# Another order inside a page step of the sample attention of a two-layer decoder step

## The chip, the cores and the metric

The kernel runs on one core of a Trainium2 chip. What is measured is the time of one execution on the device, in microseconds (us). A core has a matrix engine (TensorE, PE in the rows, with its weight loads as PEld), VectorE (DVE), ScalarE (ACT), GpSimd (POOL), and SyncE (SP), which here only issues transfers. Each of the engines runs its own list of instructions from top to bottom; they meet through semaphores.

## The reference, cut to what matters

One inference step of two decoder layers, for a prompt of 2048 tokens and for 8 sample sequences of 4 new tokens each. The change touches the sample attention of layer 0, which for every sequence reads 16 pages of 128 cached keys and values through a page table:

```python
def fox_sample(q, k_new, v_new, lf_new, k_past, v_past, lf_past):
    ...
    s_past = jnp.einsum('bqhd,bkhd->bhqk', q, k_past).astype(jnp.float32) * scale
    s_past = s_past + suf[:, :, None, :] + c_new[:, :, :, None]
    s_new = jnp.einsum('bqhd,bkhd->bhqk', q, k_new).astype(jnp.float32) * scale
    ...
    p = jax.nn.softmax(jnp.concatenate([s_past, s_new], axis=-1), axis=-1).astype(v_new.dtype)
    out = (jnp.einsum('bhqk,bkhd->bqhd', p[..., :n_past], v_past)
           + jnp.einsum('bhqk,bkhd->bqhd', p[..., n_past:], v_new))
```

There are 8 heads of width 128, so a page of keys or of values is 128 x 1024 numbers, 512 KB, and there are 128 pages of each.

## The kernel before, in words

Every large product is computed in three terms: an operand x is split into a high part, x rounded to the format of the matrix engine (`_hi`), and the low rest (`_lo`). ScalarE casts the high part, VectorE subtracts it from x for the low part.

The sample attention (`sample_fox`) does not run by itself. It is dealt out between the matrix products of a projection pass, `project_pass` with the tag p01, which multiplies half the prompt by the 41 column tiles of `fox_w_in`. A tile has two chunks of 512 tokens, a chunk four slots, and a slot is 6 matmuls of line 365; so a tile is 8 slots and 48 matmuls. After each slot every engine's program calls `beside.advance(at)`, where `at` is the position in tiles, and runs as many steps of the side works as their plans say are due. A plan is a list of (position, steps due) with straight lines between. In p01 three side works share PSUM and one after the other do their steps: `sample_gates` (14 steps), `sample_fox` (153 steps, plan (2, 0) to (32, 153)) and `prompt_memory` (42 steps, (32, 0) to (41, 42)). Each engine writes out its own list by the same rule, so the order on an engine is fixed when the program is built; when it runs is a matter of the semaphores.

A step of `sample_fox` with index i has s = i - 3. Steps i = 0 to 2 load and prepare the queries, the new keys and the masks. From s = 0 on, one page of keys goes through per step, and from s = 19 on also one page of values:

- TensorE transposes the page's keys into two PSUM banks (line 1755); ScalarE copies them out as `kT_hi` (line 1774), VectorE makes `kT_lo` (line 1840). The next page's transposes and the scores wait for `kT_lo`.
- In every second step (s even) TensorE computes the scores of the two pages before (lines 1713 and 1714), 16 matmuls; ScalarE copies half of them (`low`, line 1781), VectorE adds them up in `sc` (lines 1855 and 1858).
- ScalarE casts `v_hi` (line 1804) and VectorE makes `v_lo` (line 1886) for the page of values that the next step multiplies: they loop over `products(s + 1)`. TensorE multiplies it in step s + 1 (lines 1734 and 1735, four matmuls). `v_hi` and `v_lo` have two halves, so a cast of page y waits for the products of page y - 2 (`pv_d`).

Inside a step, TensorE's order before is scores, products, transposes; ScalarE's and VectorE's is the key split, then the work on the scores, then the value split. Once per sequence, steps 16b + 16 to 16b + 20 add the softmax (a maximum over 2052 columns, an exponential, a normalisation), the transposes of the probabilities, and the copying out of the result; the last step of a sequence multiplies two pages, the 16th and the new tokens.

In the same lists stand the evictions of the projection (ScalarE, line 382, two per tile) and the split of the next tile's weights (VectorE, lines 338 and 340, once per tile). SyncE issues the loads of key pages (ring of four), of weights, the stores of z, and in step i = 1 twenty-four small loads for masks and biases; GpSimd issues the loads of value pages (ring of three), each when the split of the page three earlier is done.

Of the kernel before, what the change touches and what calls it, by code (L numbers as in the profile page):

```python
# [14 lines left out]
P = 128  # L15
# [1542 lines left out]
def sample_fox(nc, stack, room, const, banks, zT, gate_row, bT, cache_k, cache_v, page_table, sufT, cnew, cnew_q, v_new, plan, freed):  # L1558
# [131 lines left out]
    def pe(pe):  # L1690
        for i in range(STEPS):
            s = i - LEAD
            b = batch(s, 36)
            if b is not None:
                pe.wait_ge(o_d, 2 * b + 2)
                pe.wait_ge(ptl_d, min(2 * (b + 2), 2 * DB))
                for h in range(FH):
                    last = nc.tensor.matmul(M_BANK[:, h * LO:(h + 1) * LO], o_sb[:, h * P:(h + 1) * P], eye2[:, :], start=True, stop=True)
                last.then_inc(x_d, 1)
            if group(s) is not None:  # L1700
                b, g = group(s)
                if b == 0 and g == 0:
                    pe.wait_ge(zero_d, 3)
                    pe.wait_ge(eye_d, 1)
                    pe.wait_ge(kn_d, 2)
                pe.wait_ge(qx_d, 2 * b + 2)
                pe.wait_ge(ktl_d, 2 * s)
                if s > 2:
                    pe.wait_ge(hi_d, NG * b + g + b)
                    pe.wait_ge(low_d, NG * b + g + b)  # L1710
                for h in range(FH):
                    q = qx[:, h * P:(h + 1) * P]
                    nc.tensor.matmul(S_BANK[:, 0:2 * P], q, kT_hi[:, h, :], start=(h == 0), stop=False)
                    last = nc.tensor.matmul(S_BANK[:, 0:2 * P], q, kT_lo[:, h, :], start=False, stop=(h == FH - 1))
                if g == NG - 1:
                    out = S_BANK[:, 2 * P:2 * P + TN]
                    for h in range(FH):
                        q = qx[:, h * P:(h + 1) * P]
                        nc.tensor.matmul(out, q, kn_hi[:, h, TN * b:TN * (b + 1)], start=(h == 0), stop=False)
                        last = nc.tensor.matmul(out, q, kn_lo[:, h, TN * b:TN * (b + 1)], start=False, stop=(h == FH - 1))  # L1720
                last.then_inc(s_done, 1)
            for b, p in products(s):
                y = NV * b + p
                if p == 0:
                    pe.wait_ge(ptl_d, 2 * b + 1)
                    if b:
                        pe.wait_ge(o_d, 2 * b)
                if p == PAGES:
                    pe.wait_ge(ptl_d, 2 * b + 2)
                pe.wait_ge(vl_d, y + 1)  # L1730
                pr = pT[:, p * 2 * LO:p * 2 * LO + P]
                for n in range(2):
                    vs = slice(n * 512, (n + 1) * 512)
                    nc.tensor.matmul(O_BANKS[n][:, :], pr, v_hi[:, y % 2, vs], start=(p == 0), stop=False)  # L1734
                    last = nc.tensor.matmul(O_BANKS[n][:, :], pr, v_lo[:, y % 2, vs], start=False, stop=(p == PAGES))
                last.then_inc(pv_d, 1)
            b = batch(s, 18)
            if b is not None:
                pe.wait_ge(pn_d, b + 1)
                if b >= 2:  # L1740
                    pe.wait_ge(m_d, b - 1)
                for p in range(PAGES):
                    last = nc.tensor.transpose(M_BANK[:, p * LO:p * LO + R], sc[0:R, b % 2, p * P:(p + 1) * P], ident[0:R, 0:R])
                last.then_inc(pt_d, 1)
            b = batch(s, 19)
            if b is not None:
                pe.wait_ge(ptl_d, 2 * b + 1)
                nc.tensor.transpose(M_BANK[:, 0:R], sc[0:R, b % 2, W:W + P], ident[0:R, 0:R]).then_inc(pt_d, 1)
            if 0 <= s < NPG:
                pe.wait_ge(k_in[s % KR], 16 * (s // KR + 1))  # L1750
                if s:
                    pe.wait_ge(ktl_d, 2 * s)
                for n in range(2):
                    for h in range(4):
                        last = nc.tensor.transpose(T_BANKS[n][:, h * P:(h + 1) * P], k_raw[:, s % KR, (4 * n + h) * P:(4 * n + h + 1) * P], ident[:, :])  # L1755
                    last.then_inc(kt_d, 1)
            yield

    def packed(t, first, n, off):
# [2 lines left out]
    def act(act):  # L1762
        for i in range(STEPS):
            s = i - LEAD
            if i == 1:
                act.wait_ge(set_in, 32)
                nc.scalar.activation(qs_hi[:, :, :], q_raw[:, :, :], ACT.Copy, scale=SCALE).then_inc(set_d, 1)
                act.wait_ge(zero_d, 3)
            if 0 <= s < NPG:
                for n in range(2):  # L1770
                    act.wait_ge(kt_d, 2 * s + n + 1)
                    if s % 2 == 0 and s and n == 0:
                        act.wait_ge(s_done, s // 2)
                    nc.scalar.copy(kT_hi[:, 4 * n:4 * n + 4, s % 2 * P:(s % 2 + 1) * P],  # L1774
                                   T_BANKS[n][:, :].rearrange("p (h n) -> p h n", h=4)).then_inc(kth_d, 1)
# [20 lines left out]
            if b is not None:  # L1796
                act.wait_ge(pt_d, 2 * b + 2)
                nc.scalar.copy(packed(pT, PAGES, 1, 0), M_BANK[:, 0:LO].rearrange("p (n r) -> p n r", r=LO)).then_inc(pth_d, 1)
            for b, p in products(s + 1):
                y = NV * b + p  # L1800
                act.wait_ge(v_in[y % VR], 16 * (y // VR + 1))
                if y >= 2:
                    act.wait_ge(pv_d, y - 1)
                nc.scalar.copy(v_hi[:, y % 2, :], v_raw[:, y % VR, :]).then_inc(vh_d, 1)
# [9 lines left out]
    def dve(dve):  # L1814
        def diag(off):
            return qx[:, off:off + FH * (P + TN)].rearrange("p (h x) -> p h x", x=P + TN)[:, :, 0:TN]
        for i in range(STEPS):
# [8 lines left out]
            if i == 2:  # L1826
                dve.wait_ge(kn_in, 16 * (1 + 3 * FH))
                nc.vector.tensor_copy(kn_hi[:, :, :], kn_raw[:, :, :]).then_inc(kn_d, 1)
                dve.wait_ge(kn_d, 1)
                nc.vector.tensor_tensor(kn_lo[:, :, :], kn_raw[:, :, :], kn_hi[:, :, :].bitcast(F32), ALU.subtract).then_inc(kn_d, 1)  # L1830
                nc.vector.tensor_tensor(c_bias[:, :, :], c_qry[:, :].unsqueeze(2).broadcast_to([R, DB, TN]), c_key[:, :, :], ALU.subtract).then_inc(bias_d, 1)
                dve.wait_ge(bias_d, 1)
                nc.vector.tensor_tensor(c_bias[:, :, :], c_bias[:, :, :], mask[:, :].unsqueeze(1).broadcast_to([R, DB, TN]), ALU.add).then_inc(bias_d, 1)
                dve.wait_ge(bias_d, 2)
                dve.wait_ge(set_d, 2)
            if 0 <= s < NPG:
                for n in range(2):
                    at = (slice(None), slice(4 * n, 4 * n + 4), slice(s % 2 * P, (s % 2 + 1) * P))
                    dve.wait_ge(kth_d, 2 * s + n + 1)
                    nc.vector.tensor_tensor(kT_lo[at], T_BANKS[n][:, :].rearrange("p (h n) -> p h n", h=4),  # L1840
                                            kT_hi[at].bitcast(F32), ALU.subtract).then_inc(ktl_d, 1)
# [37 lines left out]
            if b is not None:  # L1879
                dve.wait_ge(pth_d, 2 * b + 2)  # L1880
                nc.vector.tensor_tensor(packed(pT, PAGES, 1, LO), M_BANK[:, 0:LO].rearrange("p (n r) -> p n r", r=LO),
                                        packed(pT, PAGES, 1, 0).bitcast(F32), ALU.subtract).then_inc(ptl_d, 1)
            for b, p in products(s + 1):
                y = NV * b + p
                dve.wait_ge(vh_d, y + 1)
                nc.vector.tensor_tensor(v_lo[:, y % 2, :], v_raw[:, y % VR, :], v_hi[:, y % 2, :].bitcast(F32), ALU.subtract).then_inc(vl_d, 1)  # L1886
# [287 lines left out]
def decoder_step(nc, ins, outs):  # L2174
# [18 lines left out]
    with ExitStack() as s:  # L2193
# [28 lines left out]
        with ExitStack() as s0:  # L2222
# [13 lines left out]
            with ExitStack() as s1:  # L2236
                hi, lo = half_states(0, 1, s1, xp, xs, norm_pre[0])

                def works(stack, landed):
                    with ExitStack() as room:  # L2240
                        gates, ends_g = sample_gates(nc, stack, room, const, banks[2:8], z0, F_ROW, fox_b_f, past, fox_lf_s, sufT,
                                                     cnew, cnew_q, fox_k_s, fox_v_s, [(0, 0), (2, 14)])
                    with ExitStack() as room:
                        fox, ends_f = sample_fox(nc, stack, room, const, banks[2:8], z0, 3 * D + XW, bT, cache_k, cache_v, page_table,
                                                 sufT, cnew, cnew_q, fox_v_s.rearrange("b t h d -> (b t) (h d)"),
                                                 [(2, 0), (32, 153)], ends_g)
                    prompt, _ = prompt_memory(0, stack, stack, z0, 3 * D, 3 * D + XW + D, [(32, 0), (41, 42)],
                                              lambda sp: landed(sp, XQ - 1), ends_f)
                    return [gates, fox, prompt]
                project_pass(nc, "p01", banks, fox_w_in, hi, lo, z0, tiles, CHUNKS[1], STORES[1], works)  # L2250
# [49 lines left out]
```

## Time and profile before

| | before |
|---|---|
| median of 3 runs | 4248.09 us (4244.42 to 4254.1) |
| profiled execution, its own time | 4249.62 us |
| its span in the trace | 4248.1 us |
| TensorE matmul busy | 3629.0 us, 85% of the span |
| VectorE busy | 1889.8 us, 44% |
| ScalarE busy | 1317.4 us, 31% |
| GpSimd busy | 335.5 us, 8% |
| granted TensorE clock, mean of the run | 0.924 |

The span is the trace's from the first instruction to the last. Busy shares are means over stages with different limits; the pass p01 lies between about 726 and 1893 us of the span. The granted clock is a share of full speed: 1.00 is 2.4 GHz, and 0.5 is the lower of the two levels, 1.2 GHz.

### The profile page before, as it was taken

To read this page: it belongs to the slowest core of one execution; us is meant where nothing else is said; L and a number is where in the kernel's file an instruction comes from. 1 tells how busy PE (TensorE), PEld (TensorE's weight loads), DVE (VectorE), ACT (ScalarE), POOL (GpSimd) and SP (SyncE) were. 2 spreads that over 40 slices of the span, in tenths; PEclk is the share of its full clock that TensorE was granted. 3 is DMA by queue.
4 is the path that set the end of the run, shared out by engine and by line. 5 is a ranking of instruction groups with operands and counts; after the bars stand their busy time and mean duration, and the time that the engine had idled before them with its cause. 6 is when DMAs were issued, how large, how long until landed. Compare 5 with 4: busy or idle time off the path is not lost. (4 is left out here: it accounts for less than half of the span.)

```text
span 4248.1 us, 56572 instructions
## 1 busy us (share of the span) xinstructions
PE 3629.0 (85%) x19825; PEld 3133.0 (74%) x19825; DVE 1889.8 (44%) x3378; ACT 1317.4 (31%) x2438; POOL 335.5 (8%) x549
## 2 busy tenths in 40 slices
PE   5699995788888889988888888599689779997899
PEld 4699995677777677766777777488589767775687
DVE  3311323255455555445666666533321144574433
ACT  1211212244333434334545555211211144411111
POOL 0131000000000001000101111000000000122000
PEclk8799997999999999998999999799899989998899
DMA  4333332565555555322222222333222243474432
GB/s 143 93 89 108 120 97 84 164 192 179 172 174 180 184 184 180 120 96 101 99 92 89 82 82 82 106 104 108 83 91 91 89 130 113 131 223 157 133 113 76
DMA packets 385337, 523.94 MB, mean 123 GB/s; under 512 B 52855, under 2 KB 275064, under 8 KB 380495
## 3 DMA queue, kind: packets, MB, share of 16 engines
q1 hardware_dynamic: 317255, 398.72, 30.1%
q0 software_dynamic: 30624, 93.22, 6.7%
q10 hardware_dynamic: 37248, 29.37, 2.2%
q8 instruction: 112, 1.84, 0.2%
q14 instruction: 98, 0.80, 0.1%
HBM read 388.83 MB, written 132.74 MB: 123 GB/s over the span
## 5 line engine op out<-in xcount | busy, mean ns | idle before, releaser
L382 ACT ACTIVATE z_st_p<-bank 128x352 f32<-128x352 f32 (+3 forms) x325 | 167.8, 518 | 728.6 <-PE bank L365 727.9
L1333 PE MATMUL bank<-w_hi_o,b_hi_o 128*128 128x512 f32 x816 | 328.3, 402 | 70.3 <-DVE w_lo_o L1375 70.3
L1840 DVE TENSOR_TENSOR kT_lo_sf<-bank,kT_hi_sf 128x512 fp32r<-128x512 f32 x256 | 167.0, 687 | 379.6 <-ACT kT_hi_sf L1774 379.4
L365 PE MATMUL bank<-h00hi,w_hi_p 128*128 128x352 f32 x984 | 319.9, 325 | 11.3 <-DVE w_lo_p L340 7.7
L338 DVE CAST w_hi_p<-w_raw_p 128x1024 fp32r<-128x1024 f32 (+1 forms) x130 | 89.3, 687 | 529.7 <-PE bank L365 509.8
L1334 PE MATMUL bank<-w_hi_o,b_lo_o 128*128 128x512 f32 x816 | 324.1, 397 | 0.0
L1335 PE MATMUL bank<-w_lo_o,b_hi_o 128*128 128x512 f32 x816 | 323.9, 397 | 0.0
L365 PE MATMUL bank<-h00hi,w_lo_p 128*128 128x352 f32 x984 | 316.7, 322 | 0.0
L365 PE MATMUL bank<-h00lo,w_hi_p 128*128 128x352 f32 x984 | 316.6, 322 | 0.0
L1774 ACT CAST kT_hi_sf<-bank 128x512 fp32r<-128x512 f32 x256 | 140.1, 589 | 514.1 <-PE bank L1755 513.7
L365 PE MATMUL bank<-h01hi,w_hi_p 128*128 128x512 f32 x656 | 284.5, 434 | 8.9 <-DVE w_lo_p L340 8.9
L365 PE MATMUL bank<-h01lo,w_hi_p 128*128 128x512 f32 x656 | 262.5, 400 | 0.0
L365 PE MATMUL bank<-h01hi,w_lo_p 128*128 128x512 f32 x656 | 262.1, 399 | 0.0
L1333 PEld LDWEIGHTS bank<-w_hi_o,b_hi_o 128*128 128x128 f32 x816 | 156.3, 192 | 117.9 <-DVE w_lo_o L1375 44.3
L751 DVE TENSOR_TENSOR pT_lo_fa<-bank,pT_hi_fa 128x512 fp32r<-128x512 f32 (+2 forms) x320 | 194.1, 609 | 103.6 <-ACT pT_hi_fa L692 102.5
L645 PE MATMUL bank<-pT_hi_fa,v_hi_fa 128*128 128x256 f32 x576 | 182.8, 317 | 58.9 <-DVE mix_fa L726 50.6
L1734 PE MATMUL bank<-v_hi_sf,pT_sf 128*128 128x512 f32 x272 | 124.6, 458 | 107.8 <-DVE v_lo_sf L1886 107.7
L742 DVE CUSTOM_DVE_ANT_0 sc_fa<-bank,decay_fa 128x512 f32<-128x512 f32 (+2 forms) x320 | 193.3, 604 | 51.2 <-PE bank L625 26.4
L692 ACT CAST pT_hi_fa<-bank 128x512 fp32r<-128x512 f32 (+2 forms) x320 | 162.2, 515 | 145.5 <-PE bank L659 145.5
L697 ACT ACTIVATE sc_fa<-sc_fa,nm_fa 128x128 f32<-128x128 f32 (+15 forms) x128 | 154.2, 1205 | 148.6 <-DVE nm_fa L756 148.1
L365 PEld LDWEIGHTS bank<-h00hi,w_hi_p 128*128 128x128 f32 x984 | 185.6, 189 | 12.7 <-DVE w_lo_p L340 7.9
L365 PE MATMUL bank<-h10hi,w_hi_p 128*128 128x352 f32 x576 | 187.1, 325 | 7.1 <-DVE w_lo_p L340 7.1
(359 smaller groups left out, 8833.6 us busy)
## 6 DMA issues: line engine op xcount, KB each, us to landing
z<-z_st_p SPq DMA_DIRECT2D x128, 512.0 KB, 2.7
k_raw_sf<-in_cache_fox_k SPq DMA_DIRECT2D x128, 512.0 KB, 4.0
v_raw_sf<-in_cache_fox_v POOLq DMA_DIRECT2D x128, 512.0 KB, 3.9
w_raw_p<-in_fox_w_in SPq DMA_DIRECT2D x80, 512.0 KB, 5.1
b_raw_o<-bT SPq DMA_DIRECT2D x32, 768.0 KB, 7.4
w_raw_p<-in_pool_w_in SPq DMA_DIRECT2D x48, 512.0 KB, 4.7
out<-tok_fa ACTq DMA_DIRECT2D x64, 256.0 KB, 2.3
w_raw_o<-in_w_out ACTq DMA_DIRECT2D x24, 512.0 KB, 3.9
```

What stands on the lines that cost most here:

```text
L365: last = nc.tensor.matmul(out, wt[:, u, k, :], h[:, k, at0:at0 + width], start=(m == 0), stop=(m == MM - 1))
L382: nc.scalar.activation(z_st[0:rows, t % 2, at0:at0 + width], banks[n % 2][0:rows, 0:width], func).then_inc(z_read, 1)
L645: nc.tensor.matmul(out, v_hi[:, n, :], ph, start=(n == 0), stop=False)
L692: nc.scalar.copy(pT_hi[:, jt % 2, 4 * p:4 * p + nk, a * P:(a + 1) * P], T_BANKS[g % 2][:, 0:nk * P].rearrange("p (n q) -> p n q", q=P)).th ...
L697: nc.scalar.activation(sc[:, qs % NB, 0:w], sc[:, qs % NB, 0:w], ACT.Exp, bias=nm[:, qs % NB:qs % NB + 1], accum_out=rs[:, qs // QB % 2, q ...
L742: nc.vector.tensor_tensor_reduce(out=sc[:, b, k0:k0 + w], in0=S_BANKS[g % 4][:, 0:w], in1=decay[:, k0:k0 + w], scale=1.0, scalar=LOWEST, o ...
L751: nc.vector.tensor_tensor(pT_lo[at], T_BANKS[g % 2][:, 0:nk * P].rearrange("p (n q) -> p n q", q=P), pT_hi[at].bitcast(F32), ALU.subtract) ...
L1333: nc.tensor.matmul(out, bh, w_hi[:, k, cols], start=(k == 0), stop=False)
L1334: nc.tensor.matmul(out, bl, w_hi[:, k, cols], start=False, stop=False)
L1335: last = nc.tensor.matmul(out, bh, w_lo[:, k, cols], start=False, stop=(k == NK - 1))
L1774: nc.scalar.copy(kT_hi[:, 4 * n:4 * n + 4, s % 2 * P:(s % 2 + 1) * P], T_BANKS[n][:, :].rearrange("p (h n) -> p h n", h=4)).then_inc(kth_d, 1)
L1840: nc.vector.tensor_tensor(kT_lo[at], T_BANKS[n][:, :].rearrange("p (h n) -> p h n", h=4), kT_hi[at].bitcast(F32), ALU.subtract).then_inc(k ...
```

## The change

On TensorE the transposes of a step now stand between the scores and the products. On ScalarE and VectorE the split of the first page of values of `products(s + 1)` now stands at the head of the step, ahead of the key split; the second page, which there is once per sequence, stays where it was. The plans change too: the gates end at 1.8 tiles in place of 2, the three preparing steps of `sample_fox` are spread over tiles 2 to 4 and the other 150 over tiles 4 to 33, and `prompt_memory` begins at 33 in place of 32. No instruction is added or taken away.

```diff
@@ sample_fox, pe(pe): after the scores, ahead of the products
+            if 0 <= s < NPG:
+                pe.wait_ge(k_in[s % KR], 16 * (s // KR + 1))
+                if s:
+                    pe.wait_ge(ktl_d, 2 * s)
+                for n in range(2):
+                    for h in range(4):
+                        last = nc.tensor.transpose(T_BANKS[n][:, h * P:(h + 1) * P], k_raw[:, s % KR, (4 * n + h) * P:(4 * n + h + 1) * P], ident[:, :])
+                    last.then_inc(kt_d, 1)
             for b, p in products(s):
                 y = NV * b + p
...
@@ sample_fox, pe(pe): the same eight lines go from the end of the step
-            if 0 <= s < NPG:
-                pe.wait_ge(k_in[s % KR], 16 * (s // KR + 1))
...
@@ sample_fox, act(act): ahead of the key split
+            for b, p in products(s + 1)[0:1]:
+                y = NV * b + p
+                act.wait_ge(v_in[y % VR], 16 * (y // VR + 1))
+                if y >= 2:
+                    act.wait_ge(pv_d, y - 1)
+                nc.scalar.copy(v_hi[:, y % 2, :], v_raw[:, y % VR, :]).then_inc(vh_d, 1)
...
-            for b, p in products(s + 1):
+            for b, p in products(s + 1)[1:]:
...
@@ sample_fox, dve(dve): ahead of the key split
+            for b, p in products(s + 1)[0:1]:
+                y = NV * b + p
+                dve.wait_ge(vh_d, y + 1)
+                nc.vector.tensor_tensor(v_lo[:, y % 2, :], v_raw[:, y % VR, :], v_hi[:, y % 2, :].bitcast(F32), ALU.subtract).then_inc(vl_d, 1)
...
-            for b, p in products(s + 1):
+            for b, p in products(s + 1)[1:]:
...
@@ decoder_step, the plans of the side works of p01
-                                                     cnew, cnew_q, fox_k_s, fox_v_s, [(0, 0), (2, 14)])
+                                                     cnew, cnew_q, fox_k_s, fox_v_s, [(0, 0), (1.8, 14)])
...
-                                                 [(2, 0), (32, 153)], ends_g)
+                                                 [(2, 0), (4, 3), (33, 153)], ends_g)
...
-                    prompt, _ = prompt_memory(0, stack, stack, z0, 3 * D, 3 * D + XW + D, [(32, 0), (41, 42)],
+                    prompt, _ = prompt_memory(0, stack, stack, z0, 3 * D, 3 * D + XW + D, [(33, 0), (41, 42)],
```

On TensorE, a step without scores between two slots of the projection (`h01` and `w_hi_p` are the projection's operands) stood so before:

```order
L365 MATMUL bank<-h01hi,w_lo_p 128x512
L1734 MATMUL bank<-v_hi_sf,pT_sf 128x512
L1735 MATMUL bank<-v_lo_sf,pT_sf 128x512
L1734 MATMUL bank<-v_hi_sf,pT_sf 128x512
L1735 MATMUL bank<-v_lo_sf,pT_sf 128x512
L1755 MATMUL bank<-ident_const,k_raw_sf 128x128 x8
L365 MATMUL bank<-h01hi,w_hi_p 128x512
```

The same step on TensorE now:

```order
L365 MATMUL bank<-h01hi,w_lo_p 128x512
L1728 MATMUL bank<-ident_const,k_raw_sf 128x128 x8
L1742 MATMUL bank<-v_hi_sf,pT_sf 128x512
L1743 MATMUL bank<-v_lo_sf,pT_sf 128x512
L1742 MATMUL bank<-v_hi_sf,pT_sf 128x512
L1743 MATMUL bank<-v_lo_sf,pT_sf 128x512
L365 MATMUL bank<-h01hi,w_hi_p 128x512
```

The eight transposes of the page of keys have moved ahead of the four products.

On ScalarE, in the middle of a sequence, a step without scores and one with them stood so before (line 382 is an eviction of the projection):

```order
L1774 CAST kT_hi_sf<-bank 128x4x128 x2
L1804 CAST v_hi_sf<-v_raw_sf 128x1024
L1774 CAST kT_hi_sf<-bank 128x4x128 x2
L1781 COPY low_sf<-bank 32x256
L1804 CAST v_hi_sf<-v_raw_sf 128x1024
L382 ACTIVATE z_st_p<-bank 128x512
```

And two such steps there now:

```order
L382 ACTIVATE z_st_p<-bank 128x512
L1774 CAST v_hi_sf<-v_raw_sf 128x1024
L1780 CAST kT_hi_sf<-bank 128x4x128 x2
L1787 COPY low_sf<-bank 32x256
L1774 CAST v_hi_sf<-v_raw_sf 128x1024
L1780 CAST kT_hi_sf<-bank 128x4x128 x2
```

The cast of the values has moved from the end of a step to its head; VectorE's subtraction of the values moves with it.

On VectorE, at the start of `sample_fox` (`kn` is the new keys, `c_bias` the bias with the mask, lines 338 and 340 the split of a weight tile), the list was:

```order
L1828 CAST kn_hi_sf<-kn_raw_sf 128x256
L1830 TENSOR_TENSOR kn_lo_sf<-kn_raw_sf,kn_hi_sf 128x256
L1831 TENSOR_TENSOR c_bias_sf<-c_qry_sf,c_key_sf 32x32
L1833 TENSOR_TENSOR c_bias_sf<-c_bias_sf,mask_sf 32x32
L1840 TENSOR_TENSOR kT_lo_sf<-bank,kT_hi_sf 128x4x128 x4
L1846 CAST qx_sf<-qs_hi_sf 128x8x4
L1847 CAST qx_sf<-qs_lo_sf 128x8x4
L338 CAST w_hi_p<-w_raw_p 128x1024
L340 TENSOR_TENSOR w_lo_p<-w_raw_p,w_hi_p 128x1024
```

It is now:

```order
L1834 CAST kn_hi_sf<-kn_raw_sf 128x256
L1836 TENSOR_TENSOR kn_lo_sf<-kn_raw_sf,kn_hi_sf 128x256
L1837 TENSOR_TENSOR c_bias_sf<-c_qry_sf,c_key_sf 32x32
L1839 TENSOR_TENSOR c_bias_sf<-c_bias_sf,mask_sf 32x32
L338 CAST w_hi_p<-w_raw_p 128x1024
L340 TENSOR_TENSOR w_lo_p<-w_raw_p,w_hi_p 128x1024
L1850 TENSOR_TENSOR kT_lo_sf<-bank,kT_hi_sf 128x4x128 x4
L1856 CAST qx_sf<-qs_hi_sf 128x8x4
L1857 CAST qx_sf<-qs_lo_sf 128x8x4
```

A weight split now stands between the preparing step and the first key split; on TensorE, 204 matmuls of the projection stand ahead of the first page's transposes where 138 stood, and 12 between the first and the second page's transposes where 6 stood.

## Rows read from the trace of the kernel before

**Rows 1.** Windows of the span: engine busy us (instructions), granted clock, DMA share, GB/s.

```profile
800.00:900.00 100.00, 94.45 (x591) 80.61 (x591) 50.89 (x84) 39.62 (x72) 2.11 (x4) 1.00 0.57 176
900.00:920.00 20.00, 18.26 (x101) 14.83 (x100) 13.28 (x18) 8.92 (x15) 1.59 (x3) 1.00 0.76 239
900.00:1640.00 740.00, 632.01 (x3464) 523.86 (x3463) 383.85 (x540) 295.07 (x471) 59.34 (x112) 0.93 0.58 180
...
1720.00:1893.00 173.00, 164.60 (x842) 132.27 (x840) 87.72 (x145) 68.80 (x194) 16.65 (x16) 1.00 0.35 113
```

**Rows 2.** Waits of TensorE, 720 to 1893 us: total us, times, longest.

```profile
PE bank L1734 <- DVE v_lo_sf L1886: 107.7, 63, 3.3
PE bank L1755 <- DVE kT_lo_sf L1840: 15.9, 5, 14.8
...
PE bank L1755 <- DMA k_raw_sf<-in_cache_fox_k: 6.8, 1, 6.8
PE bank L942 <- ACT pr_ma L1005: 4.8, 5, 1.0
```

**Rows 3.** TensorE in order of time, 1134 to 1147.3 us: start, duration, instruction.

```profile
1134.13 1.03 PE L1755 MATMUL bank<-ident_const,k_raw_sf 128*128 128x128 f32 x8
1134.92 0.48 PE L365 MATMUL bank<-h01hi,w_hi_p 128*128 128x512 f32 x1
...
1137.76 0.28 PE L1713 MATMUL bank<-kT_hi_sf,qx_sf 128*128 128x256 f32 x1
...
1139.67 0.40 PE L1734 MATMUL bank<-v_hi_sf,pT_sf 128*128 128x512 f32 x1
...
1140.61 1.04 PE L1755 MATMUL bank<-ident_const,k_raw_sf 128*128 128x128 f32 x8
...
1145.17 0.50 PE L1734 MATMUL bank<-v_hi_sf,pT_sf 128*128 128x512 f32 x1 [2.13 <-DVE v_lo_sf L1886]
```

**Rows 4.** ScalarE in the same stretch.

```profile
1134.77 1.07 ACT L1774 CAST kT_hi_sf<-bank 128x512 fp32r<-128x512 f32 x2 [2.56 <-PE bank L1755]
1135.73 1.06 ACT L1804 CAST v_hi_sf<-v_raw_sf 128x1024 fp32r<-128x1024 f32 x1
...
1142.35 0.36 ACT L1781 COPY low_sf<-bank 32x256 f32<-32x256 f32 x1
```

**Rows 5.** VectorE in the same stretch.

```profile
1135.39 1.29 DVE L1840 TENSOR_TENSOR kT_lo_sf<-bank,kT_hi_sf 128x512 fp32r<-128x512 f32 x2 [2.34 <-ACT kT_hi_sf L1774]
...
1143.07 0.46 DVE L1855 SCALAR_TENSOR_TENSOR sc_sf<-sc_sf,c_qry_sf,bank 32x256 f32<-32x256 f32 x1
...
1143.91 1.21 DVE L1886 TENSOR_TENSOR v_lo_sf<-v_raw_sf,v_hi_sf 128x1024 fp32r<-128x1024 f32 x1
```

**Rows 6.** TensorE in order of time, 1052 to 1060 us.

```profile
1054.82 0.50 PE L1734 MATMUL bank<-v_hi_sf,pT_sf 128*128 128x512 f32 x1 [2.12 <-DVE v_lo_sf L1886]
...
1057.91 0.63 PE L365 MATMUL bank<-h01lo,w_hi_p 128*128 128x512 f32 x1
1058.34 0.63 PE L365 MATMUL bank<-h01hi,w_lo_p 128*128 128x512 f32 x1
```

**Rows 7.** TensorE, then VectorE, where the sample attention starts.

```profile
777.81 1.97 PE L1755 MATMUL bank<-ident_const,k_raw_sf 128*128 128x128 f32 x8 [6.80 <-DMA k_raw_sf<-in_cache_fox_k]
...
797.15 1.94 PE L1755 MATMUL bank<-ident_const,k_raw_sf 128*128 128x128 f32 x8 [14.80 <-DVE kT_lo_sf L1840]
...
794.62 0.29 DVE L1828 CAST kn_hi_sf<-kn_raw_sf 128x256 fp32r<-128x256 f32 x1 [18.95 <-DMA c_qry_sf<-cnew_q]
...
800.51 0.68 DVE L338 CAST w_hi_p<-w_raw_p 128x1024 fp32r<-128x1024 f32 x1
801.23 1.22 DVE L340 TENSOR_TENSOR w_lo_p<-w_raw_p,w_hi_p 128x1024 fp32r<-128x1024 f32 x1
```

**Rows 8.** Casts of the pages of values, and their loads' time to landing.

```profile
L1804 ACT CAST v_hi_sf<-v_raw_sf x136: 1027/1048/1076, 878.2 to 1697.4; 128x1024 fp32r<-128x1024 f32 x136
...
DMA to landing us min/median/max: 2.1/3.9/8.6
```

More of the change, by code:

```diff
@@ L1748, in pe @@
                 nc.tensor.transpose(M_BANK[:, 0:R], sc[0:R, b % 2, W:W + P], ident[0:R, 0:R]).then_inc(pt_d, 1)
-            if 0 <= s < NPG:
-                pe.wait_ge(k_in[s % KR], 16 * (s // KR + 1))
[L1751 to L1756, printed above, removed]
             yield
```

## The prediction

> **What bounds the kernel now.** The change touches only the pass p01, so I read that stretch. First the table of windows [rows 1]: while pages of keys and values are worked on, from 900 to 1640 us, TensorE is busy for 632.01 of 740 us, against 383.85 for VectorE and 295.07 for ScalarE, and the granted clock is 0.93. From 800 to 900 us, where mostly keys are worked on, it is busy for 94.45 of 100 us at 1.00. So TensorE is the bound, and it loses time in two ways: 108 us of standing idle, and a clock that is at times at the lower of its levels.
>
> Then the table of TensorE's waits [rows 2] says for whom it stands idle: 107.7 us in 63 waits of the value products (line 1734) for the low part of the values. The waits of line 1755, 15.9 us for VectorE (14.8 of them in one wait) and 6.8 us for a page of keys, belong to the start of the work. Together these three lines hold 130 us. Last, the order of time over two steps [rows 3 to 5] shows why: the transposes start at 1134.13, the key split keeps ScalarE from 1134.77 on and VectorE from 1135.39 on, and only behind it come the casts of the values. With a step of two slots and scores the products still start on time (1139.67); in the next step, which has one slot and no scores, they stand for 2.13 us until the subtraction that starts at 1143.91 is done.
>
> **What the lower clock costs.** After a wait of 2.12 us [rows 6] projection matmuls follow each other at 0.43 us; at full speed twelve take 2.84 us with the changeover (1134.92 to 1137.76, rows 3), 0.24 us each. 0.43 is the 1.2 GHz level, 0.24 the 2.4 GHz one. A mean clock of 0.93 over 740 us is 2 x 0.07 x 740 = 104 us at the lower level, of which, if all were work, half, 52 us, is lost. That is the upper bound of what can come back; the lower is 0. I take 30: some of the 104 us is idle, and some waits will remain.
>
> **The change in a steady step, walked with these durations** [rows 3 to 5]. Let transposes start at T. They take 0.79 us to the next instruction, products 0.94 (1139.67 to 1140.61), a slot 1.42 (half of 2.84), scores 1.91. The key split ends on ScalarE at T + 1.71 (0.64 + 1.07) and on VectorE at T + 2.55 (1.26 + 1.29).
>
> Before, the value cast follows on ScalarE (0.36 later if there is a copy of scores), and VectorE's subtraction of 1.21 after the score additions: that subtraction ends at T + 4.5 in the step shown (1143.91 + 1.21 - 1140.61), and TensorE, with one slot and no scores, is at the products at T + 0.79 + 1.42 = T + 2.2. The 2.3 between are the wait of 2.13.
>
> Now the products of step s take values split in step s - 1, so they follow the transposes at once. The next thing that can wait is the next transposes or scores, which need the key split: T + 2.55 against T + 0.79 + 0.94 + 1.42 = T + 3.15 at the earliest. 0.6 us is left. The cast at the head of the next step may start when these products end, T + 1.73, and after ScalarE's key split and copy of scores (about T + 2.1); it ends at T + 3.2. VectorE adds up scores until about T + 3.4, subtracts until T + 4.6, and would be wanted for the next key split at T + 3.15 + 1.26 = T + 4.4. It is 0.2 us late, out of 0.6. A weight split, once per tile, puts 0.68 + 1.22 = 1.9 us in front [rows 7], which makes it 2.1 us late; but the plan gives 232 slots to 150 steps, 1.55 per step, so of two neighbouring steps at least one has two slots, and its 1.42 and the 0.6 cover this but for 0.1. In the steady steps I count the wait as gone.
>
> Once per sequence it is not gone. In step 16b + 18 the first cast is for the next sequence's first page, and its buffer is free only when the products of the 16th old page are done, which TensorE does behind this very step's transposes: T + 0.79 + 0.94 = T + 1.73. The key split behind the cast then starts at T + 1.73 + 1.06 = T + 2.8 in place of T + 0.64, 2.1 us late, and with the copies and the softmax of the same steps two or three later waits of 0.3 to 0.7 us appear. I take 2.5 us per sequence, 20 us for 8; bounds 5 and 64, the latter if every second step waited 1 us as well.
>
> So of 107.7 us, 20 stay: 87.7 gained, and 30 from the clock.
>
> **The start.** The first key split on VectorE stands behind the preparing step, which waits for small loads until 794.62 [rows 7]. These are issued by SyncE when the gates' room is free, so they come hardly earlier; TensorE stood without work meanwhile. It was free of waits until 777.81 - 6.80 = 771.0. With 66 more matmuls (204 against 138) ahead of the first transposes, 15.6 us at 0.237, they start at 786.6, the page has long landed, and with 12 matmuls behind it TensorE stands at the second transposes at about 790.3. VectorE gets there after the small loads and now after a weight split too: 797.15 + 1.9 = 799.1, a wait of about 9 in place of 6.8 + 14.8. By then TensorE has done 72 matmuls more than before at the same place (66 + 6), worth 17.1 us, and is 1.9 us later: 15 us gained; bounds 5 (the small loads come 10 us later, behind the weight load and the store now ahead of them on SyncE's list) and 21.6 (no wait left).
>
> **The end.** `prompt_memory` does its 42 steps in 8 tiles in place of 9. TensorE waits there for 4.8 us on ScalarE now, and is busy for 164.60 of 173 us [rows 1, 2]. Denser steps leave less between: I add 4 us, bounds 0 and 10. The matmuls of the projection are only dealt out otherwise; no instruction is new. The loads of keys (SyncE's list) keep their place against the transposes; those of values are issued when the value split is done, whose cover is below. The earlier end of the gates' plan moves two slots of 1.42 us at most and I count nothing.
>
> **Sum.** -107.7 + 20 - 30 - 15 + 4 = -128.7 us against the profiled execution's 4249.6: 4120.9, 4121 us. That execution lies 1.5 us over the median of the runs, within their spread of 9.7 us; 0.2% or 8.5 us is about what a measurement can tell from no change.
>
> **Rivals.**
> 1. *The cast at the head holds the key split in many steps.* Against it: the walk, with 0.6 us to spare. For it: ScalarE and VectorE have evictions and weight splits in the same lists, and 0.6 us is little. If every second of 128 steps waits 1 us, 64 stay in place of 20, and half of the clock's share: -107.7 + 64 - 15 - 15 + 4 = -70, 4180 us. Decided by whether the key split ends later than T + 3.15. The Trainium skill's "TensorE: Matmul & The Clock Gate" (section "Architectural detail: the array is 16× 32×32, not 1× 128×128") says that the queues of ScalarE and VectorE are strictly first in, first out, so that nothing behind a waiting cast can pass it; it speaks for this rival. By the rule alone the sum would go to 4180; by the rows the cast waits for products that end before the next transposes start, except once per sequence, and it stays at 4121.
> 2. *The clock does not come back.* The waits go, but TensorE's dips stay, as with the 0.93 of today: 0 in place of 30, 4151 us. Against it: 1.00 from 800 to 900 us with the same instructions but the products.
> 3. *All of it comes back*: 5 us of waits left, 50 from the clock, 2 at the end: -107.7 + 5 - 50 - 15 + 2 = -166, 4084 us.
> 4. *Slower: pages of values come too late.* The load of a page is issued when the split of the page three earlier is done, and the cast at the head then holds the key split, and with it all of TensorE, until the page lands. Steps now last (1697.4 - 878.2) / 128 = 6.4 us [rows 8], afterwards some 5.5; cover is 3 x 5.5 less the cast's 1.06 and the subtraction's 1.21, 14 us. It decides from there on: with 17.5 us to landing, a step lasts 6.6, and 128 steps 26 us more, less 15 at the start and 4 back: 4265 us. Against it: loads land in 3.9, at most 8.6 us, and the engines moved 239 GB/s in one stretch, against 180 now [rows 1] and some 180 x 6.4 / 5.5 = 210 then.
>
> **Chances.** The forecast 0.55 (its own range 4095 to 4145), rival 1 0.17, rival 2 0.13, rival 3 0.11, rival 4 0.04. The predicted time is that of the forecast. The range from 4080 to 4185 takes in rivals 1 to 3 with the bounds of the waits and of the clock, and leaves out rival 4 and more waits than rival 1 has. Faster by over 0.2% are the first four cases but for a part of rival 1 that goes far beyond its price: 0.93; within 0.2% 0.03; slower 0.04.
>
> **What would show it.** In the waits of TensorE: line 1742 on `v_lo` nearly gone; some 20 us on `kT_lo` (lines 1713 and 1728), at the same steps of every sequence, and one of about 9 us at the start; nothing on pages of values by ScalarE but at the sequences' ends. The granted clock of the stretch at 0.97 or more, TensorE's busy share there at 0.95 or more. Wrong it would be made by many waits of 0.3 to 1 us on `kT_lo` (rival 1), by a clock of 0.93 without idle time (rival 2), or by ScalarE's casts waiting for loads (rival 4).

## The result, and the profile after

| | before | changed |
|---|---|---|
| median, runs taken together | 4249.83 us (4 runs, 4244.42 to 4254.1) | 4075.64 us (4 runs, 4065.68 to 4077.56) |
| ratio, 95% interval | | 0.9586 (0.9567 to 0.9605) |
| profiled execution | 4249.62 us | 4075.30 us |
| span | 4248.1 us | 4073.8 us |

The change makes the kernel 174 us faster; 4121 was predicted, in a range from 4080, so the sign is right, the size is not, and the time lies below the range.

The head of the changed kernel's page, with its span in 40 slices (granted clock and transfers):

```profile
span 4073.8 us, 56573 instructions
...
PE 3561.2 (87%) x19825; PEld 3098.8 (76%) x19825; DVE 1884.2 (46%) x3378; ACT 1320.7 (32%) x2438; POOL 336.6 (8%) x549
...
PEclk8799998899999999989999998899799799997899
...
GB/s 137 98 98 98 126 95 90 146 199 243 232 216 240 236 201 113 102 82 106 103 83 90 96 86 46 127 116 88 91 95 95 85 124 122 157 215 167 114 108 79
```

TensorE's busy time falls from 3629.0 to 3561.2 us with the same 19825 instructions. The slices from the eighth to the seventeenth are the pass p01: from the ninth on the clock is at 9, and in the ninth to the fifteenth the transfers run at 199 to 243 GB/s.

The windows table over the whole pass, of the kernel before and then of the changed one; the pass ends at 1892.0 and at 1713.3 us, so each window is the pass, rounded up to a us. The columns are those of [rows 1].

```profile
726.00:1893.00 1167.00, 1020.08 (x5489) 840.35 (x5489) 573.65 (x833) 444.78 (x791) 92.63 (x158) 0.94 0.54 167
```

```profile
726.00:1714.00 988.00, 955.40 (x5489) 808.88 (x5489) 568.04 (x832) 447.65 (x791) 93.38 (x158) 0.99 0.62 197
900.00:1640.00 740.00, 722.57 (x4218) 616.04 (x4217) 457.63 (x650) 360.35 (x610) 78.10 (x137) 1.00 0.66 210
```

This pair of rows splits the gain. The pass is 179 us shorter (1167 and 988). TensorE's idle time falls from 146.9 (1167 - 1020.08) to 32.6 us, by 114.3; its busy time for the same 5489 instructions falls by 64.7. The rest of the span, 4248.1 - 1893 and 4073.8 - 1714, is within 5 us the same. In the stretch of [rows 1] the clock goes from 0.93 to 1.00 and the busy time from 632.01 to 722.57 of 740 us.

Not all of the 64.7 us is the clock. Summed over windows of 5 us, the granted clock stands at the lower level for 128 us of the pass before and for 19 us of it now; half of the difference, 55 us, is the most that the clock can have given back. The other 10 us or so fit the ends of matmuls in front of a wait. These two rows of the kernel before stand ahead of the wait of 2.13 us in [rows 3]:

```profile
1142.41 0.39 PE L365 MATMUL bank<-h01lo,w_hi_p 128*128 128x512 f32 x1
1142.64 0.40 PE L365 MATMUL bank<-h01hi,w_lo_p 128*128 128x512 f32 x1
```

A matmul's row lasts 0.39 to 0.40 us, but the next one starts 0.23 us after it. The last one before a wait therefore counts as busy for some 0.16 us in which TensorE would already have begun the next; for the 63 waits of [rows 2] that is an estimated 10 us.

TensorE's waits in the pass, the answer to [rows 2]:

```profile
PE bank L1728 <- DVE kT_lo_sf L1850: 12.3, 6, 10.8
...
PE bank L942 <- ACT pr_ma L1005: 8.2, 9, 1.0
PE bank L1713 <- DVE qx_sf L1857: 4.4, 7, 0.8
PE bank L1742 <- DVE v_lo_sf L1896: 1.4, 1, 1.4
...
PE bank L1742 <- DVE pT_sf L1886: 1.1, 4, 0.3
```

The 107.7 us on `v_lo` are gone but for 1.4 and a 0.5 that is not shown. One wait of 10.8 us at the start is left of 21.6, and `prompt_memory` waits 8.2 in place of 4.8.

A step of one slot without scores, the kind that lost 2.13 us in [rows 3], with the scores behind it: TensorE, then VectorE.

```profile
1151.86 1.04 PE L1728 MATMUL bank<-ident_const,k_raw_sf 128*128 128x128 f32 x8
1152.65 0.48 PE L1742 MATMUL bank<-v_hi_sf,pT_sf 128*128 128x512 f32 x1
...
1153.67 0.40 PE L365 MATMUL bank<-h01hi,w_hi_p 128*128 128x512 f32 x1
...
1155.06 0.28 PE L1713 MATMUL bank<-kT_hi_sf,qx_sf 128*128 128x256 f32 x1
```

```profile
1152.26 1.23 DVE L1845 TENSOR_TENSOR v_lo_sf<-v_raw_sf,v_hi_sf 128x1024 fp32r<-128x1024 f32 x1 [1.46 <-ACT v_hi_sf L1774]
1153.40 1.28 DVE L1850 TENSOR_TENSOR kT_lo_sf<-bank,kT_hi_sf 128x512 fp32r<-128x512 f32 x2
```

The products start 0.79 us after the transposes (1152.65) because `v_lo` was made in the step before. The key split of 1.28 us that starts at 1153.40 ends at 1154.68; the slot's six matmuls start at 1153.67 and last, at 0.23 us each, until 1155.06, where the scores follow at once. 0.4 us of slack is left, and nothing waits.

### The profile page after: what moved, and what is told of

It is laid out like the page before. It is cut to its first block and busy times, and to the rows that moved or that the text cites. A ratio compares the mean times of both kernels' runs of the same rounds, so it can differ in the third digit from the quotient of the medians.

```text
span 4073.8 us, 56573 instructions
## 1 busy us (share of the span) xinstructions
PE 3561.2 (87%) x19825; PEld 3098.8 (76%) x19825; DVE 1884.2 (46%) x3378; ACT 1320.7 (32%) x2438; POOL 336.6 (8%) x549
## 5 line engine op out<-in xcount | busy, mean ns | idle before, releaser
L365 PE MATMUL bank<-h01hi,w_hi_p 128*128 128x512 f32 x656 | 269.2, 410 | 9.0 <-DVE w_lo_p L340 9.0
L659 PE MATMUL bank<-ident_const,sc_fa 128*128 128x128 f32 x1088 | 176.1, 279 | 20.6 <-ACT sc_fa L697 13.9
```

Source lines behind the costliest of these rows:

```text
L365: last = nc.tensor.matmul(out, wt[:, u, k, :], h[:, k, at0:at0 + width], start=(m == 0), stop=(m == MM - 1))
L659: last = nc.tensor.transpose(T_BANKS[g % 2][:, n * P:(n + 1) * P], sc[:, qt % NB, (4 * p + n) * P:(4 * p + n + 1) * P], ident[:, :])
```

## The experiments

Two theories. A: TensorE lost time because too little work lay between what releases a split and what needs it; either move gives the missing cover, and the clock had fallen behind those waits. The rivals: B, only the two moves together carry it; C, the clock's share has another cause, such as the plans. The pass's rows are read from windows tables as above.

| run | median us | ratio to before (95%) | pass us | TensorE busy | idle | clock 900 to 1640 |
|---|---|---|---|---|---|---|
| before | 4249.83 | 1 | 1167 | 1020.1 | 146.9 | 0.93 |
| changed | 4075.64 | 0.9586 (0.9567 to 0.9605) | 988 | 955.4 | 32.6 | 1.00 |
| plans only | 4246.99 | 0.9981 (0.9971 to 0.9990) | 1161 | 1023.8 | 137.2 | 0.93 |
| order only | 4086.04 | 0.9594 (0.9578 to 0.9610) | 1001 | 960.8 | 40.2 | 0.99 |
| transposes first only | 4100.65 | 0.9630 (0.9614 to 0.9646) | 1011 | 962.2 | 48.8 | 0.99 |
| values first only | 4107.26 | 0.9645 (0.9629 to 0.9661) | 1021 | 967.0 | 54.0 | 0.99 |
| changed, again | 4074.49 | 0.9579 (0.9566 to 0.9592) | 990 | 956.6 | 33.4 | 1.00 |
| wait in every 4th step | 4147.51 | 0.9750 (0.9732 to 0.9768) | 1066 | 975.3 | 90.7 | 0.97 |
| wait in every 2nd step | 4261.05 | 1.0019 (1.0007 to 1.0031) | 1179 | 1015.7 | 163.3 | 0.93 |

**Plans or order.** The first run is the kernel before with the three plan lines of the change, the second the changed kernel with the three plan lines of before:

```diff
@@ e1: before.py
-  [(0, 0), (2, 14)]       [(2, 0), (32, 153)]           [(32, 0), (41, 42)]
+  [(0, 0), (1.8, 14)]     [(2, 0), (4, 3), (33, 153)]   [(33, 0), (41, 42)]
@@ e2: after.py
-  [(0, 0), (1.8, 14)]     [(2, 0), (4, 3), (33, 153)]   [(33, 0), (41, 42)]
+  [(0, 0), (2, 14)]       [(2, 0), (32, 153)]           [(32, 0), (41, 42)]
```

> The kernel before with the three new plans and nothing else. Theory A (TensorE lost time to the waits for the values, and its clock fell behind these waits; the plans only save waits at the start): the wait of the value products stays at about 105 us, the granted clock of the stretch 900 to 1640 at about 0.93, only the start's 21.6 us fall to about 11; 4235 us. Rival C (the clock's gain came from the other start and the other spread of the steps): clock near 1.00 in that stretch in spite of the waits, 4190 us or less.

> The changed kernel with the three old plans: the order of the change alone. Theory A: the value waits are gone and the clock is near 1.00, while the start's waits of about 20 us are back; some 12 us over the changed kernel, 4088 us. Rival C: clock back near 0.93, 4130 us or more.

The kernel before took 4255.16 us beside these runs (median of 13). The plans alone give 8 us, the order alone 169. For the plans alone A had 4235 us, and 4246.99 was measured: TensorE's idle time fell by 9.7 us, as expected of the start, but its busy time rose by 3.7. The waits of the run with the plans alone:

```profile
PE bank L1734 <- DVE v_lo_sf L1886: 106.0, 62, 4.7
PE bank L1755 <- DVE kT_lo_sf L1840: 13.2, 5, 12.1
```

106.0 us on the values stay, and the clock stays at 0.93. C falls as far as the plans go: the clock comes back with the order and does not come back without it.

**One move at a time.** The third run moves only TensorE's transposes, the fourth only the value split:

```diff
@@ e3: after.py, act and dve as before the change
-            for b, p in products(s + 1)[0:1]:
...
-            for b, p in products(s + 1)[1:]:
+            for b, p in products(s + 1):
@@ e4: after.py, pe as before the change: the transposes go back behind the products
-            if 0 <= s < NPG:
-                pe.wait_ge(k_in[s % KR], 16 * (s // KR + 1))
...
```

> The changed kernel with ScalarE's and VectorE's order of before: only TensorE's transposes are moved. Theory A (what counts is how much TensorE has to do between the transposes, which release the splits, and the value products): moving the products behind the next transposes gives the value split 0.8 to 1.7 us more; it ends at 3.9 to 4.6 us after the start of the transposes before, and the products are reached at 3.9 us at the earliest; some 20 us of waits for v_lo stay, in steps of one slot, 4105 us. Rival B (the value split must also stand first, or the key split before it holds it): half of the waits stay, about 50 us, and half of the clock's loss, 4155 us or more.

> The changed kernel with TensorE's order of before: only the value split stands first on ScalarE and VectorE. Theory A: the value split of the next page is then done before this step's transposes release the key split, so the products never wait; the scores and the next transposes follow the transposes by 2.2 us at the earliest and need the key split at 2.55 us, so some 10 to 25 us of waits for kT_lo appear, 4100 us. Rival B (only with the transposes first is there cover): waits for kT_lo of 60 us or more, 4165 us or more.

The waits of TensorE that remain, with the transposes first only:

```profile
PE bank L1742 <- DVE v_lo_sf L1886: 24.2, 30, 2.9
```

and with the values first only:

```profile
PE bank L1713 <- DVE qx_sf L1857: 9.9, 7, 1.5
...
PE bank L1713 <- issue: 8.1, 23, 0.7
PE bank L1734 <- DVE pT_sf L1886: 7.1, 7, 1.6
```

Each move alone gives 148 to 155 us, near what A's walk gave (4105 and 4100) and far from B's 4155 and 4165. With the transposes first, 24.2 us of waits on `v_lo` are left, 20 were expected. With the values first, there are the waits that the walk did not name: on `qx`, on `pT` and on TensorE's own issue, 25 us, and only a us beside the start's on `kT_lo`, where 10 to 25 were expected. So they are two ways to the same cover, and the second of them adds some 20 to 30 us.

**Waits put back.** In the changed kernel the products of every fourth step also wait for the key split of the same step; in the second run it is every second step, with `p % 2 == 0`:

```diff
                 pe.wait_ge(vl_d, y + 1)
+                if p % 4 == 2 and s < NPG:
+                    pe.wait_ge(ktl_d, 2 * s + 2)
                 pr = pT[:, p * 2 * LO:p * 2 * LO + P]
```

> The changed kernel, in which the value products of every fourth step also wait for the key split of the same step: 32 waits of about 1.8 us, 57 us in all, put back on purpose. Theory A (the clock falls behind such waits, and before each us of wait cost 0.57 us of slower work: 64.8 us for 113.6): 57 + 32 = 89 us, 4165 us. Rival C (the clock's loss of before has another cause): 57 us, 4132 us, with the granted clock of the stretch at 0.99.

> The same in every second step: 64 waits of about 1.8 us, 115 us, as much as was taken away. Theory A: 115 + 65 = 180 us, 4255 us, with a granted clock of about 0.93. Rival C: 4190 us, with a clock of 0.99.

TensorE's waits for the key split ahead of the products, in the first and in the second run:

```profile
PE bank L1744 <- DVE kT_lo_sf L1852: 59.9, 27, 4.2
```

```profile
PE bank L1744 <- DVE kT_lo_sf L1852: 133.5, 61, 4.2
```

The windows table of the second run, the pass and the stretch, and three rows of TensorE in order of time from it:

```profile
728.00:1907.00 1179.00, 1015.66 (x5489) 848.23 (x5489) 571.34 (x833) 450.27 (x791) 92.80 (x158) 0.94 0.53 165
900.00:1640.00 740.00, 610.82 (x3383) 517.83 (x3382) 373.06 (x528) 291.13 (x457) 59.89 (x111) 0.93 0.57 180
```

```profile
1103.45 0.76 PE L1744 MATMUL bank<-v_hi_sf,pT_sf 128*128 128x512 f32 x1 [3.74 <-DVE kT_lo_sf L1852]
...
1108.28 0.63 PE L365 MATMUL bank<-h01hi,w_lo_p 128*128 128x512 f32 x1
1108.71 0.63 PE L365 MATMUL bank<-h01hi,w_hi_p 128*128 128x512 f32 x1
```

No work is added, yet TensorE is busy for 59 us more than in the changed kernel run again (1015.66 against 956.6), beside 130 us more of idle time; the clock is at 0.93 again, and behind a wait projection matmuls follow each other at 0.43 us (1108.28 and 1108.71), the 1.2 GHz level. With half as many waits it is 18.7 us beside 57.3. The median, 4261.05 us, is near A's 4255 and far from C's 4190. This is A's order of things, waits first and the clock behind them. A's price of 0.57 us per us of wait holds only for the kernel it was read from: it is 0.33 in the one run, 18.7 / 57.3, and 0.45 in the other, which is why every fourth step came out at 4147.5 us and not at 4165. By the estimate above, some 4 of the 18.7 us and 10 of the 59 are the ends of matmuls ahead of the waits; the rest goes with the clock.

**The end of a sequence, and the start.** Three value buffers let the cast at the head of a step go without waiting for products; for the room the ring of keys goes from four to three pages and the output shares the query's buffer. In the other run VectorE's wait for the small loads moves behind the first key splits, to just ahead of the first score additions:

```diff
@@ e7
-    KR, VR = 4, 3
+    KR, VR = 3, 3
-    v_hi, v_lo = (c.sb(n, [P, 2, D], F32R) for n in ("v_hi", "v_lo"))
+    v_hi, v_lo = (c.sb(n, [P, 3, D], F32R) for n in ("v_hi", "v_lo"))
+    out_all = q_raw
...
-                if y >= 2:
-                    act.wait_ge(pv_d, y - 1)
+                if y >= 3:
+                    act.wait_ge(pv_d, y - 2)
@@ e6, dve: the block from the wait on kn_in to the wait on bias_d
-            if i == 2:
+            if s == 2:
                 dve.wait_ge(kn_in, 16 * (1 + 3 * FH))
...
@@ e6, pe
-                    pe.wait_ge(kn_d, 2)
...
                 if g == NG - 1:
+                    if b == 0:
+                        pe.wait_ge(kn_d, 2)
```

> The changed kernel again, as the base for the two runs beside it: 4075 us within 0.2%.

> The changed kernel with three in place of two buffers for v_hi and v_lo, so that the cast at the head of a step never waits for the products of the step itself; for the room the ring of keys has three pages in place of four and the output shares the query's buffer. The prediction's step (at a sequence's end the head cast holds the key split, 2.5 us per sequence, 20 us): 4055 to 4060 us. Rival, by the trace of the changed kernel (the hold is covered by the second page's products and the transposes of the probabilities): no change, 4075 us within 4.

> The changed kernel, with VectorE's wait for the small loads (and the split of the new keys and the bias behind it) moved from the preparing step to just before the first score additions, and TensorE's wait for the new keys to their first use. Theory A (the wait of 10.8 us at the start is VectorE standing at the small loads ahead of the first key split): that wait goes, some of it comes back two steps later at the first scores; 4075 - 8 = 4067 us. Rival (the first key split is late for another reason, such as the key page or the weight split): no change, 4075 us.

> The kernel with the later wait for the new keys once more, because its time fell by 13 us while the pass it touches took only 3 us less. If those 13 us belong to the kernel: 4061 us within 4. If they were of that chip and hour: about 4070 us.

> Both small changes, the later wait for the new keys and three value buffers. If the two gains are separate and real (13 and 6 us): 4056 us. If only what the pass shows is real (3 and 4 us): 4067 us.

| run | median us | ratio to before (95%) | pass us | behind the pass us |
|---|---|---|---|---|
| changed, again | 4074.49 | 0.9579 (0.9566 to 0.9592) | 990 | 2354 |
| three value buffers | 4068.78 | 0.9561 (0.9548 to 0.9574) | 986 | 2356 |
| later wait | 4061.49 | 0.9548 (0.9535 to 0.9561) | 987 | 2347 |
| later wait, again | 4064.64 | 0.9560 (0.9544 to 0.9576) | 986 | 2350 |
| both | 4059.11 | 0.9549 (0.9533 to 0.9566) | 976 | 2350 |

Three buffers give 6 us, not the 15 to 20 that the hold was priced at: ScalarE's cast at a sequence's end no longer waits (1131.08) and the key split starts at the transposes (1133.16),

```profile
1131.08 1.04 ACT L1775 CAST v_hi_sf<-v_raw_sf 128x1024 fp32r<-128x1024 f32 x1
1133.16 1.08 ACT L1781 CAST kT_hi_sf<-bank 128x512 fp32r<-128x512 f32 x2 [1.03 <-PE bank L1729]
```

but the pass is only 4 us shorter, and behind the start TensorE's waits are much the same: 1.5 us on `kT_lo` in both runs, 4.4 and 4.3 us on `qx`. The intervals of the two ratios overlap, so the 6 us are little more than the runs can tell from nothing. With the later wait, the wait at the start goes from 11.5 us (changed, again) to 6.3:

```profile
PE bank L1729 <- DVE kT_lo_sf L1843: 7.8, 6, 6.3
```

What holds the 6.3 us is no longer the small loads. The weight split, which the change put ahead of the first key split on VectorE, waits for its own load:

```profile
793.15 0.69 DVE L338 CAST w_hi_p<-w_raw_p 128x1024 fp32r<-128x1024 f32 x1 [14.39 <-DMA w_raw_p<-in_fox_w_in]
...
795.02 1.28 DVE L1843 TENSOR_TENSOR kT_lo_sf<-bank,kT_hi_sf 128x512 fp32r<-128x512 f32 x2
```

So the theory and its rival each hold in part here.

Behind the pass is the span less the end of the pass's window. Both together have the lowest median, 4059.11 us, but the ratio is that of the later wait alone (0.9549 and 0.9548), so the runs do not show that the two gains add up. In the one trace of both, the pass is 14 us shorter than that of the changed kernel run again, more than the 3 or 4 of each alone. The medians of the later wait lie 10 to 13 us under the changed kernel's 4074.49, though one of the first four runs of the changed kernel also took only 4065.68; the pass accounts for 3 to 4 of them. The others lie behind the pass, in stages that the edit does not touch, where the three runs with it take 2347 to 2350 us and the other two 2354 and 2356. What does that was not found.

## Why the prediction was wrong

**What bounds the kernel**, right: waits for `v_lo`, too little cover, in the place named. The transposes-first and values-first runs show that more cover, of either kind, takes most of these waits away: 24.2 and about 3 us on `v_lo` are left of 107.7.

**The steady step**, right: 0.6 us of slack was enough. After 880 us the profile lists no wait on `kT_lo`, and VectorE's weight splits were absorbed, as in the walk.

**The sequence's end**, wrong: "I take 2.5 us per sequence, 20 us for 8". These 20 us were to be waits on `kT_lo`, and the profile lists none there; about 8 us are left in the pass on `qx`, `pT` and `v_lo` together. The mechanism is there, only hardly anybody waits for it. ScalarE, VectorE and TensorE at such a step:

```profile
1132.53 1.05 ACT L1774 CAST v_hi_sf<-v_raw_sf 128x1024 fp32r<-128x1024 f32 x1 [3.40 <-PE bank L1743]
1133.48 1.06 ACT L1780 CAST kT_hi_sf<-bank 128x512 fp32r<-128x512 f32 x2
```

```profile
1134.75 1.28 DVE L1850 TENSOR_TENSOR kT_lo_sf<-bank,kT_hi_sf 128x512 fp32r<-128x512 f32 x2
```

```profile
1130.47 1.03 PE L1728 MATMUL bank<-ident_const,k_raw_sf 128*128 128x128 f32 x8
...
1133.29 1.18 PE L1751 MATMUL bank<-ident_const,sc_sf 32*128 32x32 f32 x16
...
1137.26 1.03 PE L1728 MATMUL bank<-ident_const,k_raw_sf 128*128 128x128 f32 x8
```

The cast waits for the products until 1132.53 and the key split starts only behind it, at 1133.48, though all transposes, from 1130.47 on, are long done. The Trainium skill ("TensorE: Matmul & The Clock Gate", section "Architectural detail: the array is 16× 32×32, not 1× 128×128") states that the queues of ScalarE and VectorE are strictly first in, first out; these rows agree, 1133.48 behind 1132.53. VectorE ends the key split at 1136.03, T + 5.6 with T the start of the transposes, 3.0 us later than in the steady walk; I had 2.1. But in the same step TensorE does a second page's products, the sixteen transposes of the probabilities (1133.29) and two slots before it wants the key split, at 1137.26, T + 6.8 in place of T + 3.15. I followed the split's lateness through ScalarE and VectorE and did not lay TensorE's own extra work of the same step against it: 3.0 us late met 3.6 us more of cover and the 0.6 of slack. Where such a step has one slot, as from 958.79 to 964.50, TensorE stands idle for 0.1 us. Rival 1, the same hold in many steps, did not appear either.

**The clock**, wrong, and the larger part: "That is the upper bound of what can come back; the lower is 0. I take 30". TensorE's busy time fell by 64.7 us. Two terms were mis-sized. Of the clock's 52 nearly all came back: 128 us of the pass at the lower level became 19, and half of the difference is 55 us, in a pass of which the bound counted only 900 to 1640 us. I took little more than half, though my own walk took the waits away. The idle part was a reason to take less, but a small one: by the rows TensorE stood idle for some 16 of the 128 us. The other 10 us or so are a term that I put at nothing, the ends of the matmuls ahead of the waits; it stood in my own walk, as the 2.3 us from need to end beside a wait of 2.13. The runs with waits put back show that the slower work belongs to the waits; that the ends of matmuls are what the clock leaves over is an estimate.

**The start**, right: the first page's transposes at about 786, the second at 800.02 after a wait of 10.78 us; predicted were 786.6, 799.1 and 9. What VectorE does ahead of it, and TensorE's wait:

```profile
795.63 0.29 DVE L1834 CAST kn_hi_sf<-kn_raw_sf 128x256 fp32r<-128x256 f32 x1 [17.64 <-DMA c_qry_sf<-cnew_q]
...
797.45 1.23 DVE L340 TENSOR_TENSOR w_lo_p<-w_raw_p,w_hi_p 128x1024 fp32r<-128x1024 f32 x1
798.59 1.28 DVE L1850 TENSOR_TENSOR kT_lo_sf<-bank,kT_hi_sf 128x512 fp32r<-128x512 f32 x2
```

```profile
800.02 1.94 PE L1728 MATMUL bank<-ident_const,k_raw_sf 128*128 128x128 f32 x8 [10.78 <-DVE kT_lo_sf L1850]
```

The order without the plans is 10 us slower than the changed kernel by the medians, and its pass 13 us longer (1001 and 988); in the sum the plans stood for 15 less 4. **The end**: `prompt_memory` waits 8.2 us on ScalarE and 1.1 on VectorE in place of 4.8 and 2.5, some 2 us more; predicted 4.

In one line: idle time -114.3 where about -96 was predicted (-107.7 + 20, 12.6 less at the start, 4 more at the end), busy time -64.7 where -30 to -33 was. The nearest case was rival 3, all of it comes back, 4084 us, with a chance of 0.11; by my own walk it deserved more. Rival 4 stayed away: pages of values landed in 4.4 us in the median, at most 9.7, at 224 GB/s from 900 to 1560 us.

## What to carry to other kernels

Where an engine waits in every second step for a chain of others, ask how much of its own work lies between what starts the chain and what needs its end; here either move alone gave 148 to 155 us, and the second added some 20 to 30. Price a wait on TensorE with what follows it: here each us of idle time went with 0.3 to 0.6 us more of busy time, so count the clock over the whole stage and let it go with the waits. Where a step holds a split back, lay the bounding engine's own extra work in that step against the delay before counting a stall.

## What was not expected of the hardware

TensorE's added busy time does not grow in proportion to its added idle time: 18.7 us beside 57.3, 59 beside 130, and 64.7 beside 114.3 between the two kernels. Nor are waits of one length followed alike in the kernel before: behind the 2.12 us at 1054.82 a stretch at the 1.2 GHz level follows [rows 6], behind the 2.13 us at 1145.17 [rows 3] the granted clock is 1.00 from 1145 to 1155 us. What decides it is not settled here. With the waits on `v_lo` down to 24.2 us in 30 pieces the clock of the stretch is at 0.99.
